# Down projections of a fused two-block transformer: the high and low part of an input tile in one 512-column matmul, and the last two chunks output by output

## The chip, the cores and the metric

One core of a Trainium2 chip runs the whole program; its four compute engines (TensorE, VectorE, ScalarE, GpSimd) and the queue that issues most transfers (SyncE) run side by side and wait for each other through semaphores. The metric is the time of one execution on the device in microseconds, the median of the runs of one kernel.

## What is computed

Two transformer blocks over 256 tokens with 1024 features: attention in two kinds, cross attention to a memory, a gated feed-forward; then a layer with windowed attention and short convolutions and one with gated linear attention, each with a feed-forward and an embedding step. All is float32. The change concerns the three feed-forwards, whose inner width is 2816:

```
def swiglu(x, norm_g, w_gate, w_up, w_down):
    h = rms_norm(x, norm_g)
    return (jax.nn.silu(h @ w_gate) * (h @ w_up)) @ w_down
...
x = x + swiglu(x, ffn_norm_g[l], w_gate[l], w_up[l], w_down[l])
...
x = x + _conv_ffn(_rms_norm(x, ffn_norm[i]), ffn_w_up[i], ffn_conv_w[i], ffn_conv_b[i], ffn_w_down[i])
x = x + _per_layer_embedding(x, p[i], ple_norm[i], ple_w_gate[i], ple_w_proj[i])
```

## The kernel before

**Layout.** Activations lie features first: a tile is 128 features (partitions) by 256 tokens. x has 8 such tiles, the inner activation of a feed-forward (hid) has 22. A product is out tile += weights(128 x 128).T @ input tile, summed in a bank of the accumulator memory (PSUM; 512 columns, so a bank holds two output tiles). There are eight banks: three in a ring, g0 to g2, and d0 to d4, of which the last is called STAT.

**Precision.** Each product of two float32 operands is made of three matmuls in the split format fp32r. An operand v is kept as a high part (what ScalarE's copy rounds to) and a low part (v minus the high part, made by VectorE). The sum is high x high + high x low + low x high. So a weight block moves three matmuls of 256 columns: w_hi with the input's high part, w_hi with its low part, w_lo with its high part.

**Weights.** All weights come in 172 chunks of 1 MB (128 x 2048 elements) in one fixed order (the table PHASES, L73). Each goes through one of three slots of raw, w_hi and w_lo: SyncE loads raw; ScalarE makes w_hi (split_hi, L907), which waits until TensorE is through with the chunk three earlier; VectorE makes w_lo (split_lo, L1327); TensorE waits for lo_done. Both engines call `ahead`, which splits the chunk two ahead of the one named. TensorE adds one to chunk_done at each chunk's end.

**The order of work** is written by hand, per engine: each engine's function is a list of instructions, and what stands behind a waiting instruction on the same engine waits too. Loops over chunks (Counts.each, L104) peel three turns, roll what is left in threes, and peel the remainder.

**Down stages.** down0, down1 and down2 take 11 chunks each; a chunk holds the weights of two input tiles (h = 0, 1) for all eight output tiles f. chunk_k (L569) runs them: for ten chunks, h outside and f inside; in the last, f outside and h inside, so that banks d0 to d3 fill one after the other, each with two output tiles. The next phase is hy_in (after down0), or proj and gate (after down1 and down2, in `embedding`, L790): one chunk over k by chunk_k, then four chunks of `chunk`.

VectorE's `down` (L1603) makes the low parts of the chunks ahead, then for each of the four banks adds 512 columns to x, and between these makes the low parts of the normalised x (prep_pair, a_lo or b_lo); then the low part of the chunk two behind the stage's last, and the sums of squares. ScalarE's `down` (L1100) makes w_hi of all chunks up to that same one, then `prep` (L947) makes the high parts of x (a_hi or b_hi) and the squares, pair by pair as x_ready comes.

```
            def prep(ready, moving, gain, g0=0):
                for i in range(KT // 2):
                    act.wait_ge(ready, count.next(ready))
                    prep_pair(moving, gain, g0, x, i)
```

## Time and profile before

| | |
|---|---|
| runs | 1079.05 us median of 3 (1078.85 to 1079.26) |
| the profiled execution | 1079.18 us, span 1077.4 us |
| instructions | 21910, of them 8772 matmul records |
| TensorE busy | 1065.9 us, 99% |
| VectorE, ScalarE busy | 818.7 us (76%), 645.8 us (60%) |
| granted TensorE clock, mean | 0.998 |
| HBM read | 183.96 MB, 172 GB/s over the span |
| down0, down1, down2 | 62.66, 62.78, 62.72 us |

The profile names instructions by engine and line; a line is often a helper's (L496 is every matmul, L905 every ScalarE activation, L1315, L1318, L1321 and L1325 VectorE's multiply, add, subtract and fused operation), so the tiles written and read (out<-in) tell the stage. PE is TensorE's matmul, PEld its weight load, DVE is VectorE, ACT is ScalarE. In the views in order of time a row gives the start in us from the span's start, the duration in us, and an idle time before it with its releaser in brackets, if there was one. The duration of a matmul record includes its way through the array; what it costs in a stream is the distance from one start to the next. A float32 matmul appears as two records.

### The profile page before, as it was taken

Reading aid. Unit: us, or ns where it says so; the run is one execution under the profiler, and the core shown is the slowest. Engines: PE = TensorE matmul, PEld = TensorE weight load, DVE = VectorE, ACT = ScalarE, POOL = GpSimd, SP = SyncE. Lnnn points to the kernel's source line nnn. Section 1 sums busy time; section 2 is a strip of 40 time slices with the busy share of each in tenths; the row PEclk is TensorE's granted clock in tenths of the full one; section 3 lists DMA queues with packets and bytes.
Section 4 is the critical chain, followed back from the end, with each engine's and each line's share of the span. In section 5 each row is a group of like instructions: output and inputs, shape, how many; then the busy total and the mean of one; then the engine's idle time right before and its main releaser. Section 6 shows DMA issues by size and latency. Waiting matters only on the chain.

```text
span 1077.4 us, 21910 instructions
## 1 busy us (share of the span) xinstructions
PE 1065.9 (99%) x8772; PEld 1052.5 (98%) x8772; DVE 818.7 (76%) x1044; ACT 645.8 (60%) x898; POOL 2.7 (0%) x8
## 2 busy tenths in 40 slices
PE   7999999999999999999999999999999999999998
PEld 7999999999999999999999999999999999999998
DVE  6789875576666746898788886398998788888466
ACT  6666554355444346666787775375546587786453
POOL 0000000000000000000000000000000000000000
PEclk9999999999999999999999999999999999999999
DMA  9942462454555564534545556554332545555641
GB/s 335 252 169 79 157 234 80 157 186 176 166 186 194 182 210 157 183 126 152 196 157 193 177 184 235 195 177 160 127 120 107 180 173 189 166 199 195 224 134 73
DMA packets 30537, 187.04 MB, mean 174 GB/s; under 512 B 3735, under 2 KB 6520, under 8 KB 8840
## 3 DMA queue, kind: packets, MB, share of 16 engines
q1 hardware_dynamic: 29896, 185.05, 50.0%
q10 hardware_dynamic: 576, 1.05, 0.3%
q8 instruction: 49, 0.80, 0.3%
q14 instruction: 16, 0.13, 0.0%
HBM read 183.96 MB, written 1.34 MB: 172 GB/s over the span
## 4 chain that ended last, share of the span: by engine, by line
PE 98%; DVE 1%; DMA 0%; ACT 0%; issue 0%; SPq 0%; DVEq 0%
PE g L496 72%; PE d L496 26%; PE d L499 1%; DMA raw<-weights 0%; DVE w_lo L1321 0%; DVE b_lo L1325 0%; ACT w_hi L905 0%; DVE gla_o L1315 0%; ACT probs_t L905 0%; ACT b_hi L905 0%; DVE ple_z L1315 0%; DVE ple_mul L1315 0%; ACT ple_sig L905 0%; DVE x L1318 0%; SPq L419 0%
## 5 line engine op out<-in xcount | busy, mean ns | idle before, releaser
L1321 DVE TENSOR_TENSOR w_lo<-raw,w_hi 128x2048 fp32r<-128x2048 f32 (+1 forms) x174 | 388.8, 2236 | 75.4 <-ACT w_hi L905 74.8
L905 ACT ACTIVATE w_hi<-raw 128x2048 fp32r<-128x2048 f32 (+1 forms) x174 | 324.1, 1867 | 117.3 <-PE d L496 85.1
L496 PE MATMUL g<-a_hi,w_hi 128*128 128x256 f32 x1232 | 354.1, 287 | 6.9 <-DVE w_lo L1321 6.9
L496 PE MATMUL g<-a_lo,w_hi 128*128 128x256 f32 x1232 | 350.4, 284 | 0.0
L496 PE MATMUL g<-a_hi,w_lo 128*128 128x256 f32 x1232 | 350.4, 284 | 0.0
L496 PEld LDWEIGHTS g<-a_hi,w_hi 128*128 128x128 f32 x1232 | 237.9, 193 | 9.1 <-DVE w_lo L1321 6.9
L496 PEld LDWEIGHTS g<-a_lo,w_hi 128*128 128x128 f32 x1232 | 238.0, 193 | 0.2
L496 PEld LDWEIGHTS g<-a_hi,w_lo 128*128 128x128 f32 x1232 | 238.0, 193 | 0.0
L496 PE MATMUL g<-b_hi,w_hi 128*128 128x256 f32 x656 | 186.9, 285 | 0.2
L496 PE MATMUL g<-b_lo,w_hi 128*128 128x256 f32 x656 | 185.7, 283 | 0.0
L496 PE MATMUL g<-b_hi,w_lo 128*128 128x256 f32 x656 | 185.7, 283 | 0.0
L496 PE MATMUL d<-hid_hi,w_hi 128*128 (+1 forms) x528 | 148.8, 282 | 0.0
L496 PE MATMUL d<-hid_lo,w_hi 128*128 (+1 forms) x528 | 148.6, 282 | 0.0
L496 PE MATMUL d<-hid_hi,w_lo 128*128 (+1 forms) x528 | 148.6, 281 | 0.0
L496 PEld LDWEIGHTS g<-b_hi,w_hi 128*128 128x128 f32 x656 | 125.9, 192 | 0.8 <-DVE w_lo L1321 0.3
L496 PEld LDWEIGHTS g<-b_lo,w_hi 128*128 128x128 f32 x656 | 125.9, 192 | 0.1
L496 PEld LDWEIGHTS g<-b_hi,w_lo 128*128 128x128 f32 x656 | 125.9, 192 | 0.0
L496 PEld LDWEIGHTS d<-hid_hi,w_hi 128*128 128x128 f32 x528 | 99.4, 188 | 0.1
L496 PEld LDWEIGHTS d<-hid_lo,w_hi 128*128 128x128 f32 x528 | 99.4, 188 | 0.0
L496 PEld LDWEIGHTS d<-hid_hi,w_lo 128*128 128x128 f32 x528 | 99.4, 188 | 0.0
L905 ACT ACTIVATE conv_out<-conv_in,par 128x256 f32<-128x256 f32 x88 | 48.1, 594 | 41.3 <-DVE conv_in L1315 41.3
L1315 DVE TENSOR_TENSOR conv_in<-g,rstd 128x512 f32<-128x512 f32 x44 | 30.4, 691 | 14.9 <-PE g L496 14.7
(301 smaller groups left out, 1348.8 us busy)
## 6 DMA issues: line engine op xcount, KB each, us to landing
raw<-weights SPq DMA_DIRECT2D x168, 1024.0 KB, 4.9
bias_tab<-bias_dram SPq DMA_DIRECT2D x8, 192.0 KB, 9.8
x<-x_t ACTq DMA_DIRECT2D x4, 256.0 KB, 5.4
raw<-weights SPq DMA_DIRECT2D x4, 256.0 KB, 6.5
raw<-weights SPq DMA_DIRECT2D x2, 512.0 KB, 7.4
mem_t<-mem_t SPq DMA_DIRECT2D x1, 1024.0 KB, 9.7
out<-x SPq DMA_DIRECT2D x3, 256.0 KB, 2.2
hy_swap<-hy_qk SPq DMA_DIRECT2D x4, 128.0 KB, 5.9
```

Of the source, the lines that this page charges most:

```text
L496: return pe.matmul(out, lhsT, rhs, start=start, stop=stop, skip_group_check=True)
L499: return pe.transpose(out, src, ident[0:n, 0:n])
L905: return act.activation(out, in_, func, **kw)
L1315: return dve.tensor_tensor(out, a, b, ALU.mult)
L1321: return dve.tensor_tensor(out, a, b, ALU.subtract)
```

## The change

The inner activation becomes one tensor, hid_both [2, 22 x 256], high parts in the first half and low parts in the second, in the same 44 KB. In the down stages each output tile gets a bank of its own: columns 0 to 255 collect what the input's high part gives, 256 to 511 what the low part gives. So per input tile and output tile there is one matmul of 512 columns (w_hi with both parts) and one of 256 (w_lo with the high part). The eight banks are d0 to d3, STAT and the three of the ring g; on the ring they wait for the last outputs of the up stage, and the next phase's outputs wait for the additions to x (ring_free_at).

The first nine chunks run with h outside and f inside (down_chunk). The last two run together (down_end): f outside, then chunk, then h; TensorE gives chunk_done both of its counts at the end. VectorE adds each output tile to x in two additions of 256 columns, the second waiting for the first; it makes the low part of the chunk right behind the stage after the fourth output, and that of the one after it after three of the sums of squares are in hand. ScalarE (after_down for prep) makes the high part of that latter chunk behind the last high parts of x. The projection of the embedding keeps three matmuls of 256 columns (project).

The matmuls of a down stage go from 528 to 352. The core of the diff:

```diff
-        hid_hi = at("hid_hi", H, [FT, T], F32R)
-        hid_lo = at("hid_lo", H + 22 * KB, [FT, T], F32R)
+        hid_both = at("hid_both", H, [2, FT * T], F32R)
...
+        def down_place(name, f):
+
+            bank = (STAT, 0, 1, 2, 3)[f - 3:f - 2] if name == "down0" and f >= 3 else (0, 1, 2, 3, STAT)[f:f + 1] if name != "down0" else ()
+            if bank:
+                return D[bank[0]], bank[0], None
+            ring = (FIRST_OUT[AFTER_DOWN[name]] + (f if name == "down0" else f - 5)) % U
+            return G[ring], None, ring
...
+            def down_pass(name, c, slot, h, f, tile, first, final):
+
+                to = down_place(name, f)[0]
+                cols = slice(h * DM + f * P, h * DM + (f + 1) * P)
+                at_tile = bass.ds(tile * T, T)
+                mm(as_tiles(to[:]), w_hi[:, slot, cols], hid_both[:, :, at_tile], first, False)
+                return mm(to[:, 0:T], w_lo[:, slot, cols], hid_both[:, 0, at_tile], False, final)
+
+            def down_chunk(name, j, jm):
 
                 c, slot = j + FIRST[name], (FIRST[name] + jm) % U
...
+                opened = isinstance(j, int) and j == 0
+                pe.wait_ge(hid_split, count.next(hid_split, 2))
                 pe.wait_ge(lo_done, c + 1)
...
+                last_up = FIRST_OUT[AFTER_DOWN[name]]
+                for h in range(2):
+                    for i in range(KT):
+                        f = (i + (3 if name == "down0" else 0)) % KT
+                        if opened and h == 0:
+                            bank = down_place(name, f)[1]
+                            if bank is None:
+                                pe.wait_ge(evicted, last_up - U + (i - 5) + 1)
+                            else:
+                                acquire(bank)
+                        last = down_pass(name, c, slot, h, f, j * 2 + h, opened and h == 0, False)
                 last.then_inc(chunk_done, 1)
...
+            def down_end(name):
+
+                n = COUNT[name]
+                pe.wait_ge(hid_split, count.next(hid_split, 4))
+                pe.wait_ge(lo_done, FIRST[name] + n)
+                for f in range(KT):
+                    for j in (n - 2, n - 1):
+                        c = FIRST[name] + j
+                        for h in range(2):
+                            last = down_pass(name, c, c % U, h, f, j * 2 + h, False, j == n - 1 and h == 1)
+                    if f < KT - 1:
+                        last.then_inc(full_dve, 1)
+                    else:
+                        last.then_inc(chunk_done, 2)
...
-            def prep(ready, moving, gain, g0=0):
+            def after_down(name, moving, gain, g0=0):
                 for i in range(KT // 2):
-                    act.wait_ge(ready, count.next(ready))
-                    prep_pair(moving, gain, g0, x, i)
+                    act.wait_ge(x_ready, count.next(x_ready, 2))
+                    hi_parts(moving, 2 * i, [x[:, 2 * i + f, :] for f in range(2)], [pcol(gain, g0 + 2 * i + f) for f in range(2)])
+                    if i == KT // 2 - 1:
+                        ahead(name, COUNT[name] - 1, (COUNT[name] - 1) % U)
+                    squares(i, x)
...
-                count.each(COUNT[name] - first - 1, body)
-                for b in range(4):
-                    if b < 3:
+                count.each(COUNT[name] - first - 2, body)
+                for f in range(KT):
+                    if f < KT - 1:
                         dve.wait_ge(full_dve, count.next(full_dve))
                     else:
                         dve.wait_ge(chunk_done, FIRST[name] + COUNT[name])
-                    pair = x[:, 2 * b:2 * b + 2, :]
-                    add(pair, pair, as_tiles(D[b][:])).then_inc(x_ready, count.one(x_ready))
-                    if b > 0:
-                        prep_pair(moving, gain, g0, x, b - 1)
+                    tile, bank = x[:, f, :], down_place(name, f)[0]
+                    add(tile, tile, bank[:, T:2 * T]).then_inc(dve_own, count.one(dve_own))
+                    dve.wait_ge(dve_own, count.sent[dve_own])
+                    add(tile, tile, bank[:, 0:T]).then_inc(x_ready, count.one(x_ready))
+                    if f % 2 == 1 and f > 1:
+                        prep_pair(moving, gain, g0, x, f // 2 - 1)
+                    if f == 3:
+                        ahead(name, COUNT[name] - 2, (COUNT[name] - 2) % U)
                 dve.wait_ge(x_ready, count.sent[x_ready])
                 prep_pair(moving, gain, g0, x, 3)
+                add_squares(0, KT // 2 - 1)
                 ahead(name, COUNT[name] - 1, (COUNT[name] - 1) % U)
-                add_squares(0, KT // 2)
+                add_squares(KT // 2 - 1, KT // 2)
                 halve_squares()
```

How VectorE's instructions stand at the end of down0 before: the first row is W11's low part (the chunk right behind the stage), the last W12's; full_dve and chunk_done come from TensorE.

```order
L1321 TENSOR_TENSOR w_lo<-raw,w_hi 128x2048 [waits hi_done]
L1318 TENSOR_TENSOR x<-x,d 128x512 [waits full_dve] x2
L1325 SCALAR_TENSOR_TENSOR a_lo<-x,both_g,a_hi 128x256 [waits x_hi_done] x2
L1318 TENSOR_TENSOR x<-x,d 128x512 [waits full_dve]
L1325 SCALAR_TENSOR_TENSOR a_lo<-x,both_g,a_hi 128x256 [waits x_hi_done] x2
L1318 TENSOR_TENSOR x<-x,d 128x512 [waits chunk_done]
L1325 SCALAR_TENSOR_TENSOR a_lo<-x,both_g,a_hi 128x256 [waits x_hi_done] x2
L1325 SCALAR_TENSOR_TENSOR a_lo<-x,both_g,a_hi 128x256 [waits x_hi_done,x_ready]
L1325 SCALAR_TENSOR_TENSOR a_lo<-x,both_g,a_hi 128x256 [waits x_hi_done]
L1321 TENSOR_TENSOR w_lo<-raw,w_hi 128x2048 [waits hi_done]
```

And in the changed kernel, from the second addition of the fourth output on:

```order
L1375 TENSOR_TENSOR x<-x,d 128x256 [waits dve_own]
L1382 SCALAR_TENSOR_TENSOR a_lo<-x,both_g,a_hi 128x256 [waits x_hi_done] x2
L1378 TENSOR_TENSOR w_lo<-raw,w_hi 128x2048 [waits hi_done]
L1375 TENSOR_TENSOR x<-x,d 128x256 [waits full_dve]
L1375 TENSOR_TENSOR x<-x,d 128x256 [waits dve_own]
L1375 TENSOR_TENSOR x<-x,d 128x256 [waits full_dve]
L1375 TENSOR_TENSOR x<-x,d 128x256 [waits dve_own]
L1382 SCALAR_TENSOR_TENSOR a_lo<-x,both_g,a_hi 128x256 [waits x_hi_done] x2
L1375 TENSOR_TENSOR x<-x,d 128x256 [waits full_dve]
L1375 TENSOR_TENSOR x<-x,d 128x256 [waits dve_own]
L1375 TENSOR_TENSOR x<-x,d 128x256 [waits chunk_done]
L1375 TENSOR_TENSOR x<-x,d 128x256 [waits dve_own]
```

W11's low part has moved from ahead of all additions to behind the fourth output, and four outputs come after it. Behind them, up to W12's low part:

```order
L1382 SCALAR_TENSOR_TENSOR a_lo<-x,both_g,a_hi 128x256 [waits x_hi_done] x2
L1382 SCALAR_TENSOR_TENSOR a_lo<-x,both_g,a_hi 128x256 [waits x_hi_done,x_ready]
L1382 SCALAR_TENSOR_TENSOR a_lo<-x,both_g,a_hi 128x256 [waits x_hi_done]
L1375 TENSOR_TENSOR sq_sum<-sq_sum,sq 128x512 [waits sq_done]
L1375 TENSOR_TENSOR sq_sum<-sq_sum,sq 128x512 [waits dve_own,sq_done]
L1378 TENSOR_TENSOR w_lo<-raw,w_hi 128x2048 [waits hi_done]
L1375 TENSOR_TENSOR sq_sum<-sq_sum,newton 128x512 [waits dve_own,sq_done]
```

Two of the sums of squares now stand ahead of W12's low part. ScalarE at the same place before, W11's and W12's high parts first:

```order
L905 ACTIVATE w_hi<-raw 128x2048 [waits chunk_done,loaded2]
L905 ACTIVATE w_hi<-raw 128x2048 [waits chunk_done,loaded0]
L905 ACTIVATE a_hi<-x,both_g 128x256 [waits x_ready]
...
L905 ACTIVATE a_hi<-x,both_g 128x256 [waits x_ready]
L905 ACTIVATE a_hi<-x,both_g 128x256
L905 ACTIVATE newton<-x 128x512
```

And in the changed kernel:

```order
L959 ACTIVATE w_hi<-raw 128x2048 [waits chunk_done,loaded2]
L959 ACTIVATE a_hi<-x,both_g 128x256 [waits x_ready]
...
L959 ACTIVATE a_hi<-x,both_g 128x256 [waits x_ready]
L959 ACTIVATE a_hi<-x,both_g 128x256
L959 ACTIVATE w_hi<-raw 128x2048 [waits chunk_done,loaded0]
L959 ACTIVATE newton<-x 128x512
```

W12's high part has moved from ahead of the first high part of x to behind the last one.

## Rows read from the trace of the kernel before

**Rows 1.** The page: TensorE's busy time, and the chain that ended last
```profile
PE 1065.9 (99%) x8772; PEld 1052.5 (98%) x8772; DVE 818.7 (76%) x1044; ACT 645.8 (60%) x898; POOL 2.7 (0%) x8
...
PE 98%; DVE 1%; DMA 0%; ACT 0%; issue 0%; SPq 0%; DVEq 0%
```

**Rows 2.** TensorE's waits: us in total, times, longest
```profile
PE g L496 <- DVE w_lo L1321: 6.9, 1, 6.9
PE d L496 <- ACT probs_t L905: 0.2, 1, 0.2
```

**Rows 3.** Busy time in the three down stages, and the granted clock
```profile
358.93:421.59 62.66, 62.66 (x531) 62.66 (x529) 37.12 (x44) 27.47 (x25) 0.00 (x0) 1.00 0.57 200
639.89:702.67 62.78, 62.78 (x531) 62.73 (x529) 35.38 (x33) 29.67 (x30) 0.00 (x0) 1.00 0.58 202
981.24:1043.96 62.72, 62.72 (x530) 62.71 (x529) 35.38 (x33) 29.66 (x30) 0.00 (x0) 1.00 0.58 202
```

**Rows 4.** TensorE in time (start us, us), weights of 16 columns
```profile
737.20 0.28 PE L496 MATMUL d<-a_hi,gla_wlr_hi 128*16 128x256 f32 x1
...
738.33 0.28 PE L496 MATMUL d<-a_lo,gla_wlr_hi 128*16 128x256 f32 x1
```

**Rows 5.** TensorE in time, 64 moving columns
```profile
781.17 2.90 PE L496 MATMUL d<-gla_w 128*128 128x64 f32 x25
```

**Rows 6.** TensorE in time, float32 passes and what follows them
```profile
169.39 7.07 PE L496 MATMUL d<-mem_k,q_mem 128*128 128x256 f32 x32
176.11 0.47 PE L496 MATMUL g<-w_hi,b_hi 128*128 128x256 f32 x1
176.41 0.28 PE L496 MATMUL g<-w_lo,b_hi 128*128 128x256 f32 x1
```

**Rows 7.** TensorE in time, start of down1's chunk 1
```profile
645.64 0.36 PE L496 MATMUL d<-hid_hi,w_hi 128*128 128x256 f32 x1
645.83 0.28 PE L496 MATMUL d<-hid_lo,w_hi 128*128 128x256 f32 x1
```

**Rows 8.** VectorE in time, start of down1
```profile
640.08 0.69 DVE L1315 TENSOR_TENSOR conv_in<-g,rstd 128x512 f32<-128x512 f32 x1 [0.35 <-PE g L496]
...
643.20 2.29 DVE L1321 TENSOR_TENSOR w_lo<-raw,w_hi 128x2048 fp32r<-128x2048 f32 x1
```

**Rows 9.** VectorE in time, the end of down0
```profile
421.79 0.69 DVE L1318 TENSOR_TENSOR x<-x,d 128x512 f32<-128x512 f32 x1
422.39 1.67 DVE L1325 SCALAR_TENSOR_TENSOR a_lo<-x,both_g,a_hi 128x256 fp32r<-128x256 f32 x4
423.98 2.28 DVE L1321 TENSOR_TENSOR w_lo<-raw,w_hi 128x2048 fp32r<-128x2048 f32 x1
426.18 1.48 DVE L1318 TENSOR_TENSOR sq_sum<-sq_sum,sq 128x512 f32<-128x512 f32 x2
```

**Rows 10.** ScalarE in time, the end of down0
```profile
416.15 1.92 ACT L905 ACTIVATE w_hi<-raw 128x2048 fp32r<-128x2048 f32 x1 [3.78 <-PE d L496]
...
422.51 0.91 ACT L905 ACTIVATE a_hi<-x,both_g 128x256 fp32r<-128x256 f32 x2
```

**Rows 11.** VectorE in time, independent operations, then two in a chain
```profile
359.13 0.42 DVE L1315 TENSOR_TENSOR gate_z<-g,rstd 128x256 f32<-128x256 f32 x1 [1.82 <-PE g L496]
359.47 0.41 DVE L1315 TENSOR_TENSOR up_z<-g,rstd 128x256 f32<-128x256 f32 x1
...
370.21 0.88 DVE L1325 SCALAR_TENSOR_TENSOR rope_r<-rope_n,rope_r 128x256 f32<-128x256 f32 x2
```

**Rows 12.** TensorE in time, first matmul behind down0, and of W12
```profile
421.59 0.28 PE L496 MATMUL g<-a_hi,w_hi 128*128 128x256 f32 x1
...
427.34 0.28 PE L496 MATMUL g<-a_hi,w_hi 128*128 128x256 f32 x1
```

**Rows 13.** Busy time around the one fall of the clock (PEclk)
```profile
445.50:448.70 3.20, 3.20 (x27) 2.81 (x25) 1.42 (x3) 1.11 (x2) 0.00 (x0) 1.00 0.67 192
449.30:452.60 3.30, 3.30 (x17) 3.30 (x17) 3.30 (x3) 3.30 (x6) 0.00 (x0) 0.50 0.42 107
```

More of the change, by code:

```diff
@@ L76 @@
           ("up2", FT, 0), ("down2", FT // 2, 1), ("proj2", 1, 1), ("gate2", 4, 0)]
+AFTER_DOWN = {"down0": "hy_in", "down1": "gate1", "down2": "gate2"}
 W_IN_Q = 6
@@ L567, in turn_scale, with project @@
                 fill(STAT, last, full_dve, drained_dve)
-            def chunk_k(name, j, jm, moving, k0):
+            def project(name, moving):
+                c = FIRST[name]
+                pe.wait_ge(lo_done, c + 1)
+                for h in range(2):
+                    for f in range(KT):
+                        if h == 0 and f % 2 == 0:
+                            acquire(f // 2)
+                        to = D[f // 2][:, (f % 2) * T:(f % 2 + 1) * T]
+                        cols = slice(h * DM + f * P, h * DM + (f + 1) * P)
+                        mm(to, w_hi[:, c % U, cols], moving[0][:, h, :], h == 0 and f % 2 == 0, False)
+                        mm(to, w_hi[:, c % U, cols], moving[1][:, h, :], False, False)
+                        last = mm(to, w_lo[:, c % U, cols], moving[0][:, h, :], False, h == 1)
+                last.then_inc(chunk_done, 1)
@@ L573, in chunk_k @@
-                final = isinstance(j, int) and j == COUNT[name] - 1
+                opened = isinstance(j, int) and j == 0
+                pe.wait_ge(hid_split, count.next(hid_split, 2))
                 pe.wait_ge(lo_done, c + 1)
-                order = [(h, f) for f in range(KT) for h in range(2)] if final else [(h, f) for h in range(2) for f in range(KT)]
-                for h, f in order:
-                    if first and h == 0 and f % 2 == 0:
-                        acquire(f // 2)
-                    to = D[f // 2][:, (f % 2) * T:(f % 2 + 1) * T]
-                    cols = slice(h * DM + f * P, h * DM + (f + 1) * P)
-                    m_hi, m_lo = (tile_at(m, k0 + h) for m in moving)
-                    mm(to, w_hi[:, slot, cols], m_hi, first and h == 0 and f % 2 == 0, False)
-                    mm(to, w_hi[:, slot, cols], m_lo, False, False)
-                    last = mm(to, w_lo[:, slot, cols], m_hi, False, final and h == 1)
-                    if final and h == 1 and f in (1, 3, 5) and name[:4] == "down":
-                        fill(f // 2, last, full_dve, x_ready)
@@ L588, in chunk_k @@
-                last.then_inc(chunk_done, 1)
-                if final and name[:4] == "down":
-                    fill(3, None, None, x_ready)
+                last_up = FIRST_OUT[AFTER_DOWN[name]]
[9 more added lines that the diff above has]
+                        last = down_pass(name, c, slot, h, f, j * 2 + h, opened and h == 0, False)
@@ new lines, in down_chunk @@
+                last.then_inc(chunk_done, 1)
+            def down_end(name):
[5 more added lines that the diff above has]
+                        c = FIRST[name] + j
+                        for h in range(2):
+                            last = down_pass(name, c, c % U, h, f, j * 2 + h, False, j == n - 1 and h == 1)
[3 more added lines that the diff above has]
+                        last.then_inc(chunk_done, 2)
+                    due[x_ready] = due.get(x_ready, 0) + 1
+                    _, bank, ring = down_place(name, f)
+                    if bank is None:
+                        ring_free_at[ring] = due[x_ready]
+                    else:
+                        free_at[bank] = (x_ready, due[x_ready])
@@ L742, in ffn @@
                 outputs(f"up{layer}", moving)
-                def body(j, jm):
-                    pe.wait_ge(hid_split, count.next(hid_split, 2))
-                    chunk_k(f"down{layer}", j, jm, (hid_hi, hid_lo), j * 2)
-                count.each(COUNT[f"down{layer}"], body)
+                name = f"down{layer}"
+                count.each(COUNT[name] - 2, lambda j, jm: down_chunk(name, j, jm))
+                down_end(name)
             ffn(0, B)
@@ L1107, in body @@
                         between()
-                loop(COUNT[name] - first, body)
+                loop(COUNT[name] - first - 1, body)
             def rope_tables():
@@ L1129, in _ @@
             down(0, between=rope_tables)
-            prep(x_ready, A, both_g)
+            after_down("down0", A, both_g)
             for i in range(KT // 2):
@@ L1610, in body @@
                         between(j)
-                count.each(COUNT[name] - first - 1, body)
-                for b in range(4):
-                    if b < 3:
+                count.each(COUNT[name] - first - 2, body)
+                for f in range(KT):
+                    if f < KT - 1:
                         dve.wait_ge(full_dve, count.next(full_dve))
```

17 lines of the change are left out of this document (11 added, 6 removed).

## The prediction

> **What bounds the kernel now.** I read the page first, then TensorE's waits, then the three down stages by themselves, then the order of VectorE and ScalarE at their ends. TensorE is busy for 1065.9 of 1077.4 us, and the chain that ended last is 98% TensorE [rows 1]; its waits come to 7.1 us, of which 6.9 is the start of the kernel [rows 2]. So time is won only by a shorter stream of matmuls, and every new wait of TensorE is paid in full. The profiled execution took 1079.18 us around a span of 1077.4; the median of the runs is 1079.05, so I work against 1079.18 and take off 0.1 at the end.
>
> The down stages take 62.66, 62.78 and 62.72 us [rows 3] for 528 matmuls of 256 columns each. That is 0.1187 us for one, or 0.356 us for the three that one output tile gets from one input tile (a triple). There are 176 triples in a stage, 528 in all.
>
> **What a wider matmul costs.** 256 columns at 2.4 GHz are 0.107 us, so each matmul now pays some 12 ns over its columns. Two rows say from what. With weights of 16 columns the same 256 moving columns are spaced (738.33 - 737.20) / 10 = 0.113 us [rows 4]; with weights of 128 columns and only 64 moving, 22 records take 2.56 us with a last one of 0.27, so 0.109 us apiece [rows 5]. So streaming alone wants 0.113 and loading alone 0.11, and both at once give 0.119: the pace is set by the two together, not by columns. Where a pass has 512 cycles (float32, 256 columns at two cycles each) the load is hidden: 32 passes take 7.07 us with a last one of 0.38, so 6.69 / 31 = 0.216 us. After the last of them, which starts at 169.39 + 6.69 = 176.08, comes one matmul of 256 columns, and the next starts at 176.41: 0.33 us for a 512-cycle pass with a 256-column matmul behind it [rows 6]. That is what the new pair is, but for the number format. Its ends: 0.329 if the short matmul costs no more than with light weights (0.216 + 0.113), and 0.356, no gain, if the long one costs twice a short one. I take **0.335**, from the nearest row with 2 ns added, because [rows 4] shows the split format some nanoseconds above its columns. Gain per triple 0.021 us.
>
> Of this the Trainium skill ("TensorE: Matmul & The Clock Gate", Back-to-back issue gap) has a formula: columns at 2.4 GHz plus 2.5 ns. The trace agrees for 512 cycles (0.216) and not for 256 in a stream with loads (0.119 against 0.109); by the formula the pair would be 0.325 and the gain 16.4 us.
>
> **Inside the stages.** Down0: 176 x 0.335 = 58.96, a gain of 3.70 us. In down1 and down2 the gain of the first chunk is lost: chunk 1 waits already now for its low part, which VectorE ends at 645.49 [rows 8], and TensorE resumes at 645.64 with a first matmul whose follower comes 0.07 late [rows 7]. VectorE gets there by the work of the up stage's end, which does not get faster, so chunk 1 starts no earlier; about 0.3 us each goes. Gain there 3.38 us each, together **10.5 us**. Later chunks have room: high and low part of a chunk are ready some 4 us after its slot is free, and two chunks of 5.36 us lie in between. The new waits on the banks g cost nothing: the last up output is evicted at 640.77 [rows 8], and the sixth to eighth output tiles of the first chunk are reached at 641.6 to 642.3. Without that cover a chunk would wait some tenths. The order of the high and low part in one tile, the register arithmetic and the DMA queue don't change in kind; the chunks' loads are issued as before, one per chunk.
>
> **The end of a stage** is where the change pays. The last two chunks now go output by output (an output is full every 4 x 0.335 = 1.34 us), and both free their weight slots only at the very end. So the split of the weights two chunks behind the last (call it W12: the second chunk after down0, the first of the gate after down1 and down2; W11 is the chunk ahead of it) can begin only then: before, its high part ran at 416.15, five microseconds before the stage's end, and its low part was merely queued on VectorE until 423.98 [rows 9, 10]. And VectorE now does 16 additions of 256 columns instead of 4 of 512, with W11 in their middle.
>
> Count from S, the start of the last two chunks; the stage ends at E = S + 10.7. A 256-column operation of VectorE is followed by the next after 0.34 us if independent, 0.46 if it waits for its forerunner (0.88 for two, less 0.42) [rows 11], so an output's two additions take 0.80; a low part takes 0.40 (four from 422.39 to 423.98), a weight low part 2.20 (423.98 to 426.18) [rows 9]. VectorE starts the fourth output at S + 5.56 (full at 5.36, and 0.2 later, as 421.79 against 421.59 now [rows 9, 12]). From then on it never waits: that output 0.80, two low parts 0.80, W11 2.20, two outputs 1.60, two low parts 0.80, two outputs 1.60, four low parts 1.59, two sums of squares 1.40 (1.48, less the overlap with what follows). That is 10.79, so it reaches W12 at S + 16.35. ScalarE gets the last tile at S + 13.5, makes two high parts (0.8) and W12's high part (1.92) [rows 10], ready at S + 16.2. W12's low part ends 2.28 later, S + 18.63 = **E + 7.9**, and TensorE is at full pace 0.2 after that (0.15, and the late follower, as in [rows 7, 8]).
>
> TensorE wants W12 at the end of one chunk: E + 5.75 after down0 (421.59 to 427.34) [rows 12], and E + 5.70 after the others, where the projection's 48 matmuls run at the down stages' 0.1187. So it waits **2.4 us three times, together 7.2**. Within the first chunk after down0 it waits some 0.25 us for the low part of tile 4 (ready at S + 13.8 = E + 3.1, wanted at E + 2.9), which lies inside the 2.4. Now it waits for none of this: W12 ends at 426.26 [rows 9], 1.1 us before it is wanted. Behind W12 nothing new is late: W13 has another chunk of 5.75, and the means that the next phase needs have their cover moved with it. The work after down0 gets up to 1.5 us later against TensorE, where the trace shows 3 us and more of room.
>
> Sum: 1079.18 - 10.5 + 7.2 = 1075.9, less 0.1: **1075.8 us**. Own range 1073.4 to 1078.2, from 3 ns in the pair (1.6 us) and 0.3 us in each wait.
>
> **The rivals.**
> - *The short matmul is cheaper beside a long one.* With 0.329 the pair gains 0.027 x 528 = 14.3 us, 0.9 of it lost at the first chunks: 1079.05 - 13.4 + 7.4 = 1073.1. For it: [rows 5] load in 0.11. Against it: after the 512-cycle pass in [rows 6] the short matmul still took 0.117. By the formula of the Trainium skill above, 0.325, it would be 1071.3.
> - *The overhead goes by columns, not by instruction* (the one that ends slower). A 512-column matmul in the split format then costs 2 x 0.119 = 0.237, the pair 0.356, nothing is gained, and the waits at the three ends stay: E = S + 11.4, W12's low part at E + 7.6, 2.1 us each: 1079.05 + 6.2 = 1085.3. It decides from a pair of 0.341 on, where 528 x 0.015 no longer covers waits and first chunks. For it: no row has 512 columns in this format, and [rows 4] is above its columns by 6%. Against it: the 512-cycle passes of [rows 6] lose 3 ns over their cycles, not 6%.
> - *The waits at the ends are not there*, since VectorE or ScalarE is quicker than counted: 1079.05 - 10.5 = 1068.5. Against it: the ends are a plain sum of measured durations, 2.2 us beyond the limit.
> - *The clock falls.* Its granted level was half (1.2 GHz) in 449.3 to 452.6, soon after 3.2 us of mostly tiny matmuls (445.5 to 448.7) [rows 13]; 256 columns then are 0.213 us, and 3.3 us of it cost 3.3 x (1 - 0.119/0.213) = 1.5 us. If each wait of 2.4 us brings one such fall, 4.5 us come on top: 1080.3. Against it: TensorE works at full rate on both sides.
> - *A matmul costs its weight load alone, whatever its columns* (0.119 each, pair 0.237): 528 x 0.119 = 62.7 us less, and 7.4 of waits: 1023.8. Against it: 512 cycles took 0.216 [rows 6]. The same section of the Trainium skill gives about 131 ns per 512-column matmul in a stream with loads, which would be this case; no run here shows it.
>
> That the change doesn't do what it says is excluded: its matmuls are there, 512 and 256 wide in turn.
>
> **How the numbers follow.** Forecast 0.52, cheaper pair 0.16, by columns (or a price well on the way there) 0.13, no waits 0.10, clock 0.08, load alone 0.01. About 0.2% (2.2 us) is what a measurement can tell from no change, so faster means under 1076.9 and slower over 1081.2. The forecast's own range lies two thirds under 1076.9: 0.33 + 0.16 + 0.10 + 0.01 gives 0.60 faster; the rest of it, the clock case and 0.03 of the column case give 0.30 within 0.2%; 0.10 of the column case is slower. The range 1070.5 to 1081.0 leaves out the case without waits, the far end of the column case (0.09) and the load case, 0.2 in all.
>
> **What would show it.** Down stages of 59 us (without the ends' waits), TensorE's 512-column matmuls spaced 0.216 to 0.220 and the short ones 0.115 to 0.12; three waits of the first g (after down0 the second chunk) for w_lo on VectorE, 2.4 us each; VectorE busy without a gap from the fourth output's addition to W12. Wrong would be: a spacing near 0.237 for the long ones, waits under 1.5 us, or PEclk below full at the ends.

## The result: slower by 0.6%, and the profile after

The changed kernel takes **1085.07 us**, median of four executions (1082.89 to 1086.08), against 1078.95 for the kernel before, measured beside it. The ratio is 1.0057, 95% interval 1.0045 to 1.0068. The prediction was 1075.8, range 1070.5 to 1081.0: wrong in size and in sign. The profiled execution took 1082.89 us. Here and below a ratio is to the kernel before, measured beside it; one execution, of experiment 9, which took 1723.8 us at a mean granted clock of 0.557, is left out of its interval.

The page of the changed kernel, the span, the busy times and the chain [rows 1]:

```profile
span 1081.1 us, 20874 instructions
...
PE 1063.8 (98%) x8244; PEld 1025.4 (95%) x8244; DVE 829.6 (77%) x1080; ACT 645.3 (60%) x898; POOL 2.7 (0%) x8
...
PE 94%; DVE 4%; DMA 0%; ACT 0%; issue 0%; SPq 0%; DVEq 0%
```

TensorE is busy only 2.1 us less, and VectorE has come into the chain. TensorE's waits (us in total, times, longest) [rows 2]:

```profile
PE g L508 <- DVE w_lo L1378: 12.1, 4, 7.0
PE g L508 <- DVE b_lo L1378: 0.7, 1, 0.7
PE d L508 <- ACT probs_t L959: 0.2, 1, 0.2
```

Of the first line 7.0 is the start, as before. The other three, 5.1 together as idle time behind the last matmul's record, are the forecast waits for the second chunk behind each down stage (W12). The wait for b_lo, at the start of hy_out (the output projection of the attention in layer 1), is new. The three down stages (busy us and count of TensorE, weight loads, VectorE, ScalarE, GpSimd; clock; DMA) [rows 3]:

```profile
358.47:420.25 61.78, 61.78 (x355) 54.16 (x354) 39.34 (x52) 25.08 (x22) 0.00 (x0) 1.00 0.53 187
640.26:702.31 62.05, 62.05 (x354) 54.21 (x354) 37.60 (x41) 27.26 (x27) 0.00 (x0) 1.00 0.52 188
983.63:1045.65 62.02, 62.02 (x355) 54.19 (x354) 37.60 (x41) 27.26 (x27) 0.00 (x0) 1.00 0.54 187
```

A third of the matmuls has gone and the stages are 0.9, 0.7 and 0.7 us shorter. TensorE in time inside down0 shows why:

```profile
364.77 0.40 PE L508 MATMUL d<-hid_both,w_hi 128*128 128x512 f32 x1
365.01 0.28 PE L508 MATMUL d<-hid_both,w_lo 128*128 128x256 f32 x1
365.13 0.39 PE L508 MATMUL d<-hid_both,w_hi 128*128 128x512 f32 x1
365.35 0.28 PE L508 MATMUL d<-hid_both,w_lo 128*128 128x256 f32 x1
```

From the start of a wide matmul to the next start it is 0.24 or 0.22 us, over the stage 0.2305 in the mean, and 0.12 behind the short one. It makes no difference what the other engines do meanwhile: in the down0 of this profile the wide matmuls that ran with VectorE and ScalarE both idle took 0.2308 in the mean (16 of them), those with both busy 0.2306 (51). The pair takes 61.78 / 176 = **0.351 us**, not 0.335; the triple took 0.356.

The end of down0 on VectorE [rows 9], on ScalarE [rows 10] and on TensorE [rows 12], in time:

```profile
414.83 0.88 DVE L1375 TENSOR_TENSOR x<-x,d 128x256 f32<-128x256 f32 x2 [0.53 <-PE d L508]
...
416.42 2.28 DVE L1378 TENSOR_TENSOR w_lo<-raw,w_hi 128x2048 fp32r<-128x2048 f32 x1
418.62 1.65 DVE L1375 TENSOR_TENSOR x<-x,d 128x256 f32<-128x256 f32 x4
...
424.13 1.48 DVE L1375 TENSOR_TENSOR sq_sum<-sq_sum,sq 128x512 f32<-128x512 f32 x2
425.53 2.29 DVE L1378 TENSOR_TENSOR w_lo<-raw,w_hi 128x2048 fp32r<-128x2048 f32 x1
```
```profile
423.48 1.90 ACT L959 ACTIVATE w_hi<-raw 128x2048 fp32r<-128x2048 f32 x1
```
```profile
420.25 0.28 PE L508 MATMUL g<-a_hi,w_hi 128*128 128x256 f32 x1
...
425.92 0.28 PE L508 MATMUL g<-a_hi,w_lo 128*128 128x256 f32 x1
427.87 0.39 PE L508 MATMUL g<-a_hi,w_hi 128*128 128x256 f32 x1 [1.67 <-DVE w_lo L1378]
428.09 0.28 PE L508 MATMUL g<-a_lo,w_hi 128*128 128x256 f32 x1
```

VectorE has no gap from the fourth output's additions (414.83) to the low part of W12, which ends at 427.75, and TensorE stands from 426.04 (a usual distance of 0.12 behind the start at 425.92) to 427.87: 1.83 us, and 0.1 for the late follower. After down1 and down2 it is 1.86 and 1.93.

A loss that the prediction did not have lies in the up stages of layers 1 and 2. The kernel before and then the changed one, in up1 and up2 (1056 matmuls each, counted back from the down stage):

```profile
512.45:639.89 127.44, 127.44 (x1059) 127.33 (x1057) 110.83 (x150) 99.52 (x152) 0.00 (x0) 1.00 0.52 183
854.31:981.24 126.93, 126.93 (x1059) 126.88 (x1058) 110.83 (x150) 99.56 (x152) 0.00 (x0) 1.00 0.53 184
```
```profile
512.04:640.26 128.22, 128.22 (x1058) 127.22 (x1057) 110.86 (x150) 99.52 (x152) 0.00 (x0) 1.00 0.50 181
855.98:983.63 127.65, 127.65 (x1059) 127.24 (x1057) 110.91 (x150) 99.57 (x152) 0.00 (x0) 1.00 0.52 183
```

They are 0.78 and 0.72 us longer with the same work on each engine. VectorE's groups in up1 (busy, mean ns | idle before them), before and changed, show one difference beside the wait for TensorE:

```profile
L1315 DVE TENSOR_TENSOR conv_in<-g,rstd 128x512 f32<-128x512 f32 x21 | 14.5, 691 | 6.8 <-PE g L496 6.6
L1321 DVE TENSOR_TENSOR hid_lo<-conv_hid,hid_hi 128x256 f32 x17 | 7.2, 425 | 4.1 <-DVE conv_hid L1315 4.1
```
```profile
L1372 DVE TENSOR_TENSOR conv_in<-g,rstd 128x512 f32<-128x512 f32 x21 | 14.5, 691 | 6.1 <-PE g L508 6.0
L1378 DVE TENSOR_TENSOR hid_both<-conv_hid,hid_both 128x256 f32 x17 | 7.2, 425 | 5.6 <-DVE conv_hid L1372 5.6
```

The low part of the hidden state starts 0.33 us behind the end of its forerunner instead of 0.24 (in up2 0.26 instead of 0.17). VectorE's program has one register operation more there: output and input of the subtraction now lie at two offsets of one tensor, where before one offset served two tensors. In the loop of the changed kernel:

```
L1372 TENSOR_TENSOR conv_hid<-conv_gelu,conv_out 128x256
L1378 ISA
L1378 REGISTER_ALU
L1378 TENSOR_TENSOR hid_both<-conv_hid,hid_both 128x256
```

The profile has both register operations in front of the subtraction, where the kernel before has only the first. What it costs TensorE shows at the start of every second chunk of up1, where a weight low part ends just before it is wanted. VectorE and TensorE in the changed kernel:

```profile
544.44 2.28 DVE L1378 TENSOR_TENSOR w_lo<-raw,w_hi 128x2048 fp32r<-128x2048 f32 x1
```
```profile
546.66 0.28 PE L508 MATMUL g<-a_hi,w_lo 128*128 128x256 f32 x1
546.86 0.38 PE L508 MATMUL g<-a_hi,w_hi 128*128 128x256 f32 x1
```

The chunk's first matmul follows the end of the low part (546.72) by 0.14 and its forerunner by 0.20; in the kernel before it followed at the usual 0.12.

**The sum**, from the starts of matmuls in the two profiled executions: down stages -2.3, the three waits +5.9 with their followers, b_lo +0.6 (a gap of 0.94 where there was one of 0.30), up stages +1.5, together +5.7. The execution of before had one fall of the clock [rows 13], the changed one had none before its last 2 us (-1.5), and the part ahead of down0 differs by 0.5 from one execution to another: 5.7 - 1.5 - 0.5 = 3.7, the difference of the spans (1077.4 and 1081.1).

### The profile page after: what moved, and what is told of

It reads as the page before. It is cut to its first block, busy times and chain, and to the rows that moved or that the text cites. A ratio compares the mean times of both kernels' runs of the same rounds, so it can differ in the third digit from the quotient of the medians.

```text
span 1081.1 us, 20874 instructions
## 1 busy us (share of the span) xinstructions
PE 1063.8 (98%) x8244; PEld 1025.4 (95%) x8244; DVE 829.6 (77%) x1080; ACT 645.3 (60%) x898; POOL 2.7 (0%) x8
## 4 chain that ended last, share of the span: by engine, by line
PE 94%; DVE 4%; DMA 0%; ACT 0%; issue 0%; SPq 0%; DVEq 0%
PE g L508 77%; PE d L508 17%; DVE w_lo L1378 1%; DVE x L1375 1%; PE d L511 1%; DVE b_lo L1382 1%; DMA raw<-weights 0%; DVE sq_sum L1375 0%; DVE a_lo L1382 0%; ACT b_hi L959 0%; ACT hy_probs_t L959 0%; ACT w_hi L959 0%; DVE gla_o L1372 0%; ACT probs_t L959 0%; ACT hy_att L959 0%
## 5 line engine op out<-in xcount | busy, mean ns | idle before, releaser
L508 PE MATMUL d<-hid_both,w_hi 128*128 (+1 forms) x330 | 118.5, 394 | 0.0
L508 PE MATMUL d<-hid_both,w_lo 128*128 (+1 forms) x330 | 93.3, 283 | 0.0
L508 PEld LDWEIGHTS d<-hid_both,w_hi 128*128 128x128 f32 x330 | 62.0, 188 | 14.6 <-issue 0.5
L508 PE MATMUL g<-hid_both,w_hi 128*128 (+1 forms) x198 | 71.9, 393 | 0.0
L508 PEld LDWEIGHTS d<-hid_both,w_lo 128*128 128x128 f32 x330 | 62.0, 188 | 0.0
L508 PE MATMUL g<-hid_both,w_lo 128*128 (+1 forms) x198 | 56.0, 283 | 0.0
L508 PEld LDWEIGHTS g<-hid_both,w_hi 128*128 128x128 f32 x198 | 37.2, 188 | 8.6
```

The costliest lines, as they stand in the source:

```text
L508: return pe.matmul(out, lhsT, rhs, start=start, stop=stop, skip_group_check=True)
```

## The experiments

**1. Only the last chunk output by output.** The slots are freed chunk by chunk, so ScalarE makes W12's high part inside the last chunk; VectorE's low part of W12 stands ahead of the sums of squares.

```
-                    for j in (n - 2, n - 1):
+                    for j in (n - 1,):
...
-                        last.then_inc(chunk_done, 2)
+                        last.then_inc(chunk_done, 1)
...
-                add_squares(0, KT // 2 - 1)
                 ahead(name, COUNT[name] - 1, (COUNT[name] - 1) % U)
-                add_squares(KT // 2 - 1, KT // 2)
+                add_squares(0, KT // 2)
```

> The changed kernel, but only the last chunk goes output by output, and each chunk frees its weight slots at its own end, so W12's high part is made during the last chunk again. Theory A (the ends cost 2 us each in waits and the falls of the clock come from them; a pair is 0.351 us and gains 0.005 on a triple): no wait over 0.5 us at the three ends, clock at 0.998 or above in all runs, time 1079.0 - 528 x 0.005 = 1076.3 us, within 1 us. Rival B (the banks, the additions in two halves or the wide matmul itself cost what was lost): still 1082 or more.

Measured: 1083.52 us, ratio 1.0042 (1.0028 to 1.0056). A miss of 7 us, with a time in Rival B's range. The down stages kept 61.78 to 62.09, and VectorE was still late: sixteen additions fall into one chunk of 5.6 us and run without a gap to W12.

```profile
416.04 2.45 DVE L1373 TENSOR_TENSOR x<-x,g 128x256 f32<-128x256 f32 x6 [2.01 <-PE g L508]
...
425.51 2.28 DVE L1376 TENSOR_TENSOR w_lo<-raw,w_hi 128x2048 fp32r<-128x2048 f32 x1
```

TensorE waited 0.7 us for a_lo and 0.3 for W12 behind down0, and 1.2 us for W12 behind down1 and down2. The longer up stages stayed too (128.24 and 128.09). Against the changed kernel the like executions are 1.2 us shorter (1081.70 at a mean clock of 1.0, 1082.89 at 0.999). So the early freed slot alone takes away only a part of the waits; at this end too the additions, whose columns are doubled by one output per bank, keep VectorE late.

**2. The new layout and ends with matmuls of 256 columns.**

```
-                mm(as_tiles(to[:]), w_hi[:, slot, cols], hid_both[:, :, at_tile], first, False)
+                mm(to[:, 0:T], w_hi[:, slot, cols], hid_both[:, 0, at_tile], first, False)
+                mm(to[:, T:2 * T], w_hi[:, slot, cols], hid_both[:, 1, at_tile], False, False)
```

> The changed kernel with the 512-column matmul undone into two of 256 columns into the two halves of the same bank; ends, banks and additions as changed. Theory A: triples back at 0.356, so 2.6 us slower than the changed kernel in like executions (1085.1 + 2.6 = 1087.7, by 1086 to 1089), with the same three waits of about 2 us, a little shorter since the stage's end comes later. Rival B, with the wide matmul as the culprit: at or under 1082.

Measured: 1085.54 us, ratio 1.0065 (1.0049 to 1.0082), under the 1086 to 1089 expected, since it had fewer falls of the clock than the changed kernel; down stages 62.67, 62.83 and 62.82, waits of 1.8 to 1.9 as before. Three of its four executions had a full clock throughout and took 1085.3 to 1085.6, against 1082.89 for the changed kernel's profiled one, the only one of its executions with a clock as full: the wide matmul is worth 2.5 us in all, which is Theory A's term.

**3. W11's low part earlier**, after the first output's addition instead of the fourth's.

```
-                    if f == 3:
+                    if f == 0:
```

> The changed kernel with VectorE making W11's low part behind the first output's addition instead of the fourth's. VectorE's queue then has room before the last output. Theory A: VectorE reaches W12 about 1.6 us earlier, but W12's high part on ScalarE becomes the last to be ready (last addition at E + 1.1, two high parts 0.8, high part 1.9, low part 2.3: E + 6.1 against 5.7 wanted), so waits of 0.4 to 0.7 us instead of 2.0 and about 4 us off the time, 1081 or less, fewer falls of the clock. Rival: the queue isn't what ends last, waits stay near 2 us and the time within 1 us of 1085.

Measured: 1080.37 us, ratio 1.0014 (1.0004 to 1.0024). TensorE's waits were 0.57, 0.62 and 0.62 us. A hit, and the first that shows the waits as an order of work that can be mended. Only the place of ScalarE is not as expected: behind down0 W12's high part was ready at 424.94, and VectorE, still adding sums of squares, began the low part at 425.09, so the two ended almost together.

**4. The price of width.** High and low part side by side in one run; the wide matmul has 512, 384 and 320 columns in down0, down1 and down2. With fewer columns parts of the products are left out.

```
-        hid_both = at("hid_both", H, [2, FT * T], F32R)
+        hid_both = at("hid_both", H, [FT * 2 * T], F32R)
...
-                mm(as_tiles(to[:]), w_hi[:, slot, cols], hid_both[:, :, at_tile], first, False)
+                n = {"down0": 512, "down1": 384, "down2": 320}[name]
+                mm(to[:, 0:n], w_hi[:, slot, cols], hid_both[:, bass.ds(tile * 2 * T, n)], first, False)
```

> High and low part of an input tile lie side by side, so the wide matmul reads one run and writes one run; its width is 512 in down0, 384 in down1 and 320 in down2 (there part of the low part's product is left out, so the result isn't the reference's). The price of a wide matmul, from one start to the next: if the split format costs by the column (231/512 = 0.451 ns), 0.231, 0.173, 0.144; if each pays a fixed 18 ns over its columns at 2.4 GHz, 0.231, 0.178, 0.151; if the second run of 256 columns cost it, 0.216 at 512 here, 0.163 and 0.136.

Measured: 1069.68 us. TensorE in time in down1 (384) and down2 (320):

```profile
669.94 0.34 PE L508 MATMUL d<-hid_both,w_hi 128*128 x1
670.12 0.28 PE L508 MATMUL d<-hid_both,w_lo 128*128 x1
```
```profile
1009.74 0.30 PE L508 MATMUL g<-hid_both,w_hi 128*128 x1
1009.88 0.28 PE L508 MATMUL g<-hid_both,w_lo 128*128 x1
```

In the mean of the stages 0.2305 for 512, 0.180 for 384 and 0.143 for 320. Two separate runs of columns are not the cost, since one run took the same. Per column it is 0.450, 0.470 and 0.448 ns; 256 columns with light weights took 0.113 [rows 4], or 0.443. So 320 columns cost what the price by the column says (0.144), but 384 more than it says (0.173) and about what the fixed sum of 18 ns says (0.178); the price is not quite a straight line, and why is open.

**5. The price by kind.** All matmuls of down0 and down1 have 512 columns, those of down0 with weights of 16 columns. (Its expectation says 256 for the short one of down0; the kernel moved 512 there too. The parts lie side by side as in experiment 4.)

```
+                light = name == "down0"
+                n = {"down0": 512, "down1": 512, "down2": 128}[name]
+                rows = slice(0, 16 if light else P)
+                cols = slice(cols.start, cols.start + 16) if light else cols
+                mm(to[rows, 0:n], w_hi[:, slot, cols], hid_both[:, bass.ds(tile * 2 * T, n)], first, False)
+                return mm(to[rows, 0:n], w_lo[:, slot, cols], hid_both[:, bass.ds(tile * 2 * T, n)], False, final)
```

> A measurement of one price: high and low part of the hidden state lie side by side. In down0 the wide matmul of 512 columns and the short one of 256 have weights of 16 columns (only 16 rows of each output are computed); in down1 both matmuls of a pair run over 512 columns; in down2 both run over 128 columns, so half of the products are left out. The output is not the reference's. Theory (the price goes by the column that moves, 0.45 ns each, whatever the weights): 0.230 us for 512 columns with light weights too (and 0.113 for 256, as in the kernel before), 0.230 for each matmul of down1, so 0.461 a pair; 128 columns would cost 0.058 and the stage is bound by its loads or by VectorE. Rival (the wide matmul pays for the next one's full weight load, or for the change between two lengths): 0.216 to 0.220 with light weights, or 0.216 to 0.220 where both lengths are the same. Another rival: a fixed cost of about 0.012 us a matmul above 0.417 ns a column: that is 0.225 for 512 columns anywhere, and 0.066 for 128.

Measured in down0, TensorE in time:

```profile
379.80 0.40 PE L508 MATMUL g<-hid_both,w_hi 128*16 128x512 f32 x1
380.03 0.39 PE L508 MATMUL g<-hid_both,w_lo 128*16 128x512 f32 x1
```

352 matmuls took 81.55 us in down0 and 81.89 in down1: 0.232 and 0.233 apiece. Neither a light load nor an equal neighbour makes 512 columns cheaper, and the fixed surcharge (0.225) is out as well. In down2 the clock stood at 1.2 GHz from 1029.5 on and a matmul of 128 columns took 0.213; those before, at 2.4 GHz, took 0.109 to 0.115, about the 0.109 of 64 columns [rows 5], so at these widths the columns don't set the price.

**6. The layout alone**, in the kernel before: one tensor for both parts, everything else as it was.

```
-        hid_hi = at("hid_hi", H, [FT, T], F32R)
-        hid_lo = at("hid_lo", H + 22 * KB, [FT, T], F32R)
+        hid_both = at("hid_both", H, [2, FT * T], F32R)
...
-                sub(tile_at(hid_lo, j), ring[:, jm % U, :], tile_at(hid_hi, j).bitcast(F32)).then_inc(hid_split, 1)
+                sub(hid_at(1, j), ring[:, jm % U, :], hid_at(0, j).bitcast(F32)).then_inc(hid_split, 1)
```

> The kernel before, with one thing changed: the high and low parts of the hidden state lie in one tensor hid_both instead of two, as in the changed kernel; the down projections keep their three matmuls of 256 columns and their ends. VectorE needs one more register operation in front of the first of every three subtractions that make a low part of the hidden state, since both operands now lie at different offsets of one tensor. Theory: this is what lengthened the up stages of layers 1 and 2 in the changed kernel, by 0.6 and 0.65 us, and nothing else comes from it: up stages 1 and 2 with a mean pace of 5.84 us a chunk instead of 5.80, the whole 1.2 us longer than before (1078.6 where before is 1077.4, 1080.4 where it is 1079.2), down stages at 62.7, no waits at their ends. Rival: the longer up stages come from the five matmuls' rings and banks of the changed down stages, or from the state in which their late ends leave the prefetch of weights; then this kernel is the kernel before within 0.3 us.

Measured: 1080.77 us, ratio 1.0013 (1.0004 to 1.0023), so +1.6 us. Up stages 1 and 2 and VectorE's group in up1:

```profile
511.97:640.61 128.64, 128.56 (x1059) 127.52 (x1057) 111.37 (x150) 99.53 (x152) 0.00 (x0) 1.00 0.53 181
855.09:982.71 127.62, 127.62 (x1059) 127.28 (x1057) 110.88 (x150) 99.55 (x152) 0.00 (x0) 1.00 0.53 182
```
```profile
L1324 DVE TENSOR_TENSOR hid_both<-conv_hid,hid_both 128x256 f32 x17 | 7.2, 425 | 5.6 <-DVE conv_hid L1318 5.6
```

The loss is the layout's; it came out 0.4 us larger than expected, in up1 (128.64 where the changed kernel had 128.22). One thing in the expectation was wrong: in these loops the register operation stands in front of every such subtraction; only in up0, whose last 22 chunks took 126.9 us in both kernels, in front of one in three.

**7. The ends mended**, with the wide matmuls kept. W11 as in 3, W12's low part ahead of the sums of squares as in 1, and on ScalarE:

```
+                    if i == KT // 2 - 1:
+                        ahead(name, COUNT[name] - 1, (COUNT[name] - 1) % U)
                     act.wait_ge(x_ready, count.next(x_ready, 2))
                     hi_parts(moving, 2 * i, [x[:, 2 * i + f, :] for f in range(2)], [pcol(gain, g0 + 2 * i + f) for f in range(2)])
-                    if i == KT // 2 - 1:
-                        ahead(name, COUNT[name] - 1, (COUNT[name] - 1) % U)
```

> The changed kernel with the three down stages' ends put in another order: the low part of the last chunk but one is made after the first output's addition; ScalarE makes the high part of the second chunk behind the stage ahead of the last pair's high parts, and VectorE its low part directly after the last pair's low parts, ahead of all sums of squares. Theory (a term for each cause): the three waits fall from 2.0 to at most 0.15 us each, nothing takes their place, since the work moved back has more than 2 us of room; 5.6 us faster than the changed kernel: about 1077.2 where no clock fall comes, 1079 where one comes, ratio 0.998 to 1.001 to the kernel before. So the wide matmul's 2.3 to 2.5 us are eaten by the up stages' 1.25 and the wait for b_lo of 0.6. Rival: the waits are only moved: the statistics of the normalisation then come late, and TensorE waits for rstd or for a free g bank by 1 us or more at each end (1080 or more).

Measured: 1078.46 us, ratio 0.9994 (0.9985 to 1.0003). The first of TensorE's waits (the start) and the end of down0 on VectorE:

```profile
PE g L508 <- DVE w_lo L1378: 7.0, 1, 7.0
```
```profile
422.91 0.88 DVE L1382 SCALAR_TENSOR_TENSOR a_lo<-x,both_g,a_hi 128x256 fp32r<-128x256 f32 x2 [0.81 <-ACT a_hi L959]
423.71 2.28 DVE L1378 TENSOR_TENSOR w_lo<-raw,w_hi 128x2048 fp32r<-128x2048 f32 x1
425.91 1.48 DVE L1375 TENSOR_TENSOR sq_sum<-sq_sum,sq 128x512 f32<-128x512 f32 x2
```

All three waits are gone and nothing took their place; the one for b_lo is gone as well, though this profile had a fall of the clock at 448.1, ahead of its place. What is left of the change is then -2.3 for the matmuls and +1.5 for the layout, -0.8; the medians differ by -0.7.

**8. The changed kernel once more**, for the clock.

> The changed kernel as it is, once more, to see where the granted clock falls. Of its four executions so far one had a mean clock of 0.999 at 1082.9 us and three 0.996 to 0.998 at 1084.6 to 1086.1. Theory: each fall to 1.2 GHz takes 3.4 us and costs 1.6 to 1.8 us, and comes behind one of the waits at the ends of the down stages; an execution with a mean of 0.996 shows two of them and is 3.3 us longer than one without. Rival: the longer executions have longer waits elsewhere, and the stretches between the waits are not equal.

Measured: 1085.77 us. Its matmuls stand where those of the first profile stand, 0.2 us earlier, except for two places behind which they come later:

```profile
710.40:713.80 3.40, 3.40 (x19) 3.40 (x18) 2.59 (x2) 2.31 (x2) 0.00 (x0) 0.50 0.84 301
1055.20:1058.60 3.40, 3.40 (x18) 3.40 (x18) 2.65 (x3) 2.39 (x2) 0.00 (x0) 0.51 0.87 296
```

The clock is at 1.2 GHz for 3.4 us, from about 0.6 us behind the end of the waits after down1 and down2, and what follows is late by 1.5 us each time. The five executions of the changed kernel order themselves so: mean clock 0.999 at 1082.89, 0.998 at 1084.62, 0.996 at 1085.5 to 1086.1.

**9 and 10. VectorE's loop written out** over the chunks of up1 and up2, so that no register operation is left in it, in the kernel of experiment 7 (e5_ends_mended below) and in the kernel before. Experiment 9 is e7 below.

```
-                count.each(FT, body, 4)
+                count.each(FT, body, FT)
```

> The kernel of e5_ends_mended, with VectorE's loop over the 22 chunks of the up stages of layers 1 and 2 written out, so that every address and count there is a constant and no register operation stands between VectorE's instructions. Theory: these two stages run at the pace at which VectorE makes low parts, and the register operations are part of that pace: 5.84 us a chunk with the changed layout against 5.80 before. Without any of them the pace falls to TensorE's own, 48 matmuls of 0.1195 us, 5.74 to 5.76, so each stage becomes 1.5 us shorter and the whole about 1075.5 (ratio 0.996 to 0.998), faster than the kernel before. Rival: the pace is set by something else (the loads, ScalarE), or the longer code costs as much as it saves: then the time is that of e5_ends_mended, 1078.5, within 0.3 us, or above.

> The kernel before, with the same loop written out. Theory: its pace of 5.80 us in the up stages of layers 1 and 2 also falls to 5.74 to 5.76, which gives 0.9 us for each, 1.8 in all (1077.3 where before is 1079.1); e7 then lies 2.3 us or somewhat less below it, by what the wide matmul gives, since the changed layout costs nothing any more. Rival as in e7: no difference to the kernel before.

Measured: 1076.09 us, ratio 0.9973 (0.9963 to 0.9984), and 1078.76 us, ratio 0.9997 (0.9988 to 1.0006). Experiment 9 is 2.4 us under experiment 7: 1.2 and 0.8 in the up stages and 0.3 in down1 and down2 together. Up stages and VectorE's group in up1 for experiment 9, then the same for 10:

```profile
511.20:638.27 127.07, 127.06 (x1058) 126.83 (x1057) 110.90 (x150) 99.50 (x152) 0.00 (x0) 1.00 0.51 184
852.01:978.91 126.90, 126.90 (x1059) 126.85 (x1057) 110.89 (x150) 99.50 (x152) 0.00 (x0) 1.00 0.52 184
```
```profile
L1378 DVE TENSOR_TENSOR hid_both<-conv_hid,hid_both 128x256 fp32r<-128x256 f32 x18 | 7.7, 426 | 2.2 <-DVE conv_hid L1372 0.5
```
```profile
511.97:638.93 126.96, 126.96 (x1059) 126.89 (x1057) 110.99 (x150) 99.51 (x152) 0.00 (x0) 1.00 0.53 184
...
638.93:702.23 63.30, 63.30 (x530) 63.30 (x529) 35.41 (x33) 29.70 (x30) 0.00 (x0) 1.00 0.57 200
```

Both kernels now run the up stages in the same 126.9 to 127.1 us, so the layout costs nothing once its register operations are gone, and experiment 9, a changed kernel, beats the kernel before by 0.3% and experiment 10, which has the same loop, by 2.7 us. Of experiment 10 I expected 1.8 us and got 0.3: up1 is only 0.5 shorter than before, up2 was already at TensorE's pace (126.93), and down1 became 0.5 longer, 0.1199 us a matmul instead of 0.1189, all through the stage, so 0.5 of the 2.7 is not the wide matmul's. Why its matmuls run slower there is open.

## Why the prediction was wrong, step by step

- **The pair (failed).** "I take 0.335, from the nearest row with 2 ns added": it is 0.351. The step fell with the 512-cycle passes of [rows 6]: they show 0.42 ns a cycle for float32, and I read them as the price of 512 columns in the split format. Experiments 4 and 5 show that 512 columns of this format take 0.45 ns each (0.2305 to 0.233 us), with light weights and with full ones, in one run of columns or two, beside a short matmul or an equal one. The gain is 2.3 us (2.5 by experiment 2), where 10.5 stood in the sum. The clue was in [rows 4]: 0.113 us for 256 columns is 0.443 ns each. I had put the nanoseconds above 0.107 down as a sum per matmul.
- **The lost gain of the first chunks** (0.3 each in down1 and down2) went the way that was forecast, at 0.2: the stages are 0.3 longer than down0, but they were 0.1 longer before too. (With the rows' own lengths of down1 and down2 [rows 3] the gain there is 3.5 each and not 3.38, the sum 10.7; against what was measured that changes nothing.)
- **The three waits (held; 2.4 was 0.4 too high).** Cause, place and order of work came out as written: from the fourth output to W12 VectorE took 10.70 us (414.83 to 425.53) where the sum had 10.79. TensorE lost 1.9 to 2.0 us each time. The dearer pair explains most of the difference: the stage ends later against VectorE, as the rival by columns had it (2.1).
- **"The order of the high and low part in one tile, the register arithmetic and the DMA queue don't change in kind" (failed).** The arithmetic did change, and cost 1.5 us (experiments 6, 9 and 10). The program's order showed the extra operation beforehand, and I priced it at nothing without naming its cover: the VectorE work of an up chunk is only just done when TensorE wants it (546.72 for 546.86 above).
- **New waits on the banks g at nothing** held; none appears. **The 3 us of room for the work after down0** held for the statistics; for b_lo, at hy_out, TensorE lost 0.6 us. That wait appears in the five profiles with full clock around 450 us (changed kernel twice, experiments 2, 4 and 5) and in none with the fall there. So it may be a trade for that fall, which holds TensorE back by 1.5 us some 36 us ahead of it, and not a cost of the change; no profile of the kernel before without the fall exists to tell.
- **The clock.** "If each wait of 2.4 us brings one such fall" is half right. Experiment 2 had waits of 1.9 us and a full clock in three of four executions; the waits of 2.8 and 3.3 us in experiment 4 both had a fall behind them; the changed kernel, by its mean clocks, had two falls in three of five executions. At 1.5 us each they would account for its spread of 3.2 us, and the 0.6 us by which the medians differ beyond the 5.5 of executions without a fall.
- **The rivals.** "The overhead goes by columns" forecast 1085.3 at a chance of 0.13, with a turning point at a pair of 0.341. The chip took the price by columns at 0.351, with waits of 1.9. That the total lies so near is partly chance: that rival gave the matmuls no gain at all, and had neither the register operations nor the falls. Its price was the only other end that a row in this format supported, and it deserved more than a quarter of the forecast's chance.

The Trainium skill ("TensorE: Matmul & The Clock Gate", Back-to-back issue gap) gives columns at 2.4 GHz plus 2.5 ns for an isolated matmul, 0.216 us for 512 columns, and about 131 ns for 512 columns in a stream with weight loads. Measured in this format were 0.2305 in the pair and 0.232 to 0.233 in a stream of its own. The measurement decides against both.

## What to carry to other kernels

Price an operation from a row in its own number format, and divide by the column before calling the rest a cost per instruction. Merging matmuls that are bound by their columns saves little, here 5 ns per pair, and that has to pay for everything the merge needs elsewhere: here twice the columns to add (16 additions of 256 for 4 of 512), slots freed later, and an address register. Before a change that moves operands into one tensor, look whether a loop on the pace-setting engine gets another register operation; and after a change that loses, look whether its waits are only an order of work, as these were.

## What the runs showed of the hardware that I had not expected

- A matmul in the split float32 format costs 0.448 to 0.470 ns a column from 320 to 512 columns, not 0.417. Against weights of 16 columns, full weights add 5 to 6 ns at 256 columns (0.113 to 0.119) and nothing at 512 (0.232, 0.233).
- One more register operation ahead of a VectorE instruction costs about 0.09 us (idle time 0.24 to 0.33 us in up1, 0.17 to 0.26 in up2), and without any the same instruction follows after 0.10 (17 of the 18 in experiment 9; with the last the mean is 2.2 / 18 = 0.12).
- The same 0.6 us wait and 3.4 us fall of the clock sit at fixed places of the program but come or stay away from one execution to the next. In experiment 9 executions with and without a fall differ by 0.2 us only, where those of the kernel before differ by 1.8 (medians 1077.37 and 1079.14); I can't say why.
